# Feed-forward products moved 512 columns at a time, index queries rotated by ScalarE copies, and the recurrence's last steps one weight piece later

## The reference

```python
def swiglu(x, w_gate, w_up, w_down):            # 1024 -> 2816 -> 1024
    return (jax.nn.silu(x @ w_gate) * (x @ w_up)) @ w_down

# in each of the two last layers
q, k, v, ga, iq, ik, iw, xr, gr, ma, mb = jnp.split(h @ w_in[l], offsets, axis=-1)
iq = apply_rope(iq.reshape(B, S, 16, 64), cos_i, sin_i)   # [x1*c - x2*s, x2*c + x1*s]
ik = apply_rope(ik, cos_i, sin_i)
# index scores of iq and ik choose the keys of the attention
hr = rg_lru(causal_depthwise_conv_2(xr), ...)   # a recurrence over the tokens
y_b = (hr * jax.nn.silu(gr)) @ w_out_rnn[l]
merged = jax.nn.sigmoid(ma) * y_a + jax.nn.sigmoid(mb) * y_b
```

## Time and profile before

| | |
|---|---|
| median of 3 runs | 2159.14 us (2158.46 to 2160.78) |
| the profiled execution | 2158.18 us |
| its span in the trace | 2156.3 us |
| PE busy | 2111.6 us, 98% of the span |
| DVE, ACT, POOL busy | 1730.8, 1487.3, 394.1 us |
| TensorE clock granted | full in all 40 slices of the page |

### The profile page before, as it was taken

One profiled execution on the slowest core, in us unless ns is written; L12 is line 12 of the kernel. 1 busy time (PEld: TensorE's weight loads), 2 busy tenths in 40 slices (PEclk: granted clock), 3 DMA queues, 4 the chain that ended last, 5 costly groups with the idle time before them and its releaser, 6 DMA issues.

```text
span 2156.3 us, 33385 instructions
## 1 busy us (share of the span) xinstructions
PE 2111.6 (98%) x13067; PEld 1839.3 (85%) x13067; DVE 1730.8 (80%) x2150; ACT 1487.3 (69%) x1986; POOL 394.1 (18%) x354
## 2 busy tenths in 40 slices
PE   8999999989999999999999999999999999999998
PEld 8888999878888888888888888878899888999877
DVE  6756555879999999999999999985699666689775
ACT  5644444666887888888888888864578845468964
POOL 1511000001011000000000000000658600367820
PEclk9999999999999999999999999999999999999999
DMA  8225956429999999999999999985656465555561
GB/s 284 97 68 129 276 179 183 158 101 359 353 370 387 395 387 393 383 389 378 385 357 393 374 388 377 375 318 166 181 169 194 150 230 178 172 179 177 172 209 61
DMA packets 297421, 564.62 MB, mean 262 GB/s; under 512 B 19600, under 2 KB 113576, under 8 KB 297256
## 3 DMA queue, kind: packets, MB, share of 16 engines
q1 hardware_dynamic: 285328, 527.60, 69.3%
q0 software_dynamic: 11824, 34.77, 5.8%
q10 hardware_dynamic: 104, 0.04, 0.0%
HBM read 548.32 MB, written 14.02 MB: 261 GB/s over the span
## 4 chain that ended last, share of the span: by engine, by line
PE 75%; POOL 11%; DVE 4%; issue 4%; ACT 2%; DMA 2%; SPq 1%; POOLq 0%; DVEq 0%; ACTq 0%
PE bank L951 23%; PE bank L953 23%; PE bank L952 23%; POOL work L910 5%; POOL work L914 3%; PE bank L957 2%; POOL work L905 2%; DMA work<-in_w_ig_dram 1%; PE bank L1128 1%; DVE parts L2845 1%; POOL work L896 1%; DMA raw<-in_a_w_in_dram 0%; POOL work L894 0%; DVE work L2984 0%; DVE cols L2899 0%
## 5 line engine op out<-in xcount | busy, mean ns | idle before, releaser
L2845 DVE TENSOR_TENSOR parts<-raw,parts 128x1024 fp32r<-128x1024 f32 x701 | 851.1, 1229 | 307.7 <-ACT parts L2094 282.9
L2094 ACT CAST parts<-raw 128x1024 fp32r<-128x1024 f32 x701 | 731.0, 1047 | 411.7 <-PE bank L953 387.5
L951 PE MATMUL bank<-cols,parts 128*128 128x256 f32 x1376 | 398.8, 290 | 0.0
L952 PE MATMUL bank<-cols,parts 128*128 128x256 f32 x1376 | 389.8, 283 | 0.0
L953 PE MATMUL bank<-cols,parts 128*128 128x256 f32 x1376 | 389.8, 283 | 0.0
L2845 DVE TENSOR_TENSOR fast<-raw,fast 128x1024 fp32r<-128x1024 f32 x302 | 361.5, 1217 | 24.7 <-ACT fast L2094 7.7
L2094 ACT CAST fast<-raw 128x1024 fp32r<-128x1024 f32 x302 | 316.3, 1052 | 84.4 <-PE bank L953 77.0
L951 PE MATMUL bank<-parts,cols 128*128 128x512 f32 x868 | 344.2, 397 | 3.2 <-DVE cols L2899 1.9
L953 PE MATMUL bank<-parts,cols 128*128 128x512 f32 x868 | 338.5, 390 | 0.0
L952 PE MATMUL bank<-parts,cols 128*128 128x512 f32 x868 | 338.2, 390 | 0.0
L951 PEld LDWEIGHTS bank<-cols,parts 128*128 128x128 f32 x1376 | 263.7, 192 | 6.1 <-issue 4.6
(11 more groups left out here) (454 smaller groups left out, 3066.7 us busy)
## 6 DMA issues: line engine op xcount, KB each, us to landing
raw<-in_moe_w_gate_dram SPq DMA_DIRECT2D x112, 1024.0 KB, 9.0
raw<-in_moe_w_up_dram SPq DMA_DIRECT2D x112, 1024.0 KB, 8.5
raw<-in_moe_w_down_dram SPq DMA_DIRECT2D x112, 1024.0 KB, 9.1
raw<-in_w_in_dram SPq DMA_DIRECT2D x76, 1024.0 KB, 5.3
raw<-in_a_w_in_dram SPq DMA_DIRECT2D x11, 1024.0 KB, 11.7
raw<-in_ffn_w_gate_dram SPq DMA_DIRECT2D x11, 1024.0 KB, 5.4
raw<-in_ffn_w_up_dram SPq DMA_DIRECT2D x11, 1024.0 KB, 5.4
raw<-in_ffn_w_down_dram SPq DMA_DIRECT2D x11, 1024.0 KB, 5.2
```

The source lines that it names most:

```text
L951: pe.matmul(o, l[0], r[0], start=start, stop=False)
L952: pe.matmul(o, l[0], r[1], start=False, stop=False)
L2094: a.copy(dst[0], src).then_inc(*up(o + "hi", x))
L2845: v.tensor_tensor(dst[1], src, dst[0].bitcast(F32), ALU.subtract).then_inc(*up(o + "lo", x))
```

## The change

Three edits.

1. **Feed-forward.** XT's two parts are laid side by side (`XT_both`, 8 x 512 columns). Per row block there is one product of the high weights with all 512 columns and one of the low weights with the 256 high columns. Gate and up get a bank each (`N2.banks`). DVE adds the two halves of each bank (`tensor_reduce`, event `h_sum`) into SBUF; silu and the multiplication read SBUF; rounding (`h_hi`) and low part (`h_lo`) move behind the next block's first piece. The first block keeps its products.
2. **Index queries.** PE's `rope` and DVE's `rope` go. ACT makes four copies of 32 partitions per pair (`index_swaps`), driven by the pairs of the iq pieces, DVE uses `swapped`. The exchange matrix loses its sign, the sine tables get it (two more small DVE operations, once). The side task keeps its number of steps, so the index scores stand at the same steps.
3. **Recurrence.** `behind_mb` ticks behind (0, 2), (1, 0), (1, 2), (1, 3), on PE, ACT and DVE.

```diff
-    XT = tuple(v3(cols_[:, i, :], 8) for i in range(2))
+    XT_both = v3(cols_[:, :, :].rearrange("p a b -> p (a b)"), 8)
+    XT = tuple(XT_both[:, :, i * T:(i + 1) * T] for i in range(2))
...
-    N2.sg = v3(take(2 * T), 2)
+    N2.sg, N2.up = v3(take(2 * T), 2), v3(take(2 * T), 2)
...
+    N2.banks = lambda nb, q: 4 + 2 * (nb % 2) + q
...
-                b = 4 + nb % 4
                 if nb == 0:
-                    two_by_parts(0, b, *T_gu[0])
+                    two_by_parts(0, 4, *T_gu[0])
+                    busy[4] = ("h", 0)
                 for q in range(2 if nb else 0):
                     x = T_gu[nb][q]
                     _, w = piece_view(W, x)
+                    b = N2.banks(nb, q)
                     pe.wait_ge(*at(lo_name(x), x))
-                    if q == 0:
-                        claim(b)
+                    claim(b)
                     for k in range(8):
-                        k_ = mm3(bank[b][:, q * T:(q + 1) * T], sl(w, ALL, k), sl(XT, ALL, k), k == 0, k == 7)
+                        pe.matmul(bank[b][:, :], w[0][:, k], XT_both[:, k, :], start=k == 0, stop=False, skip_group_check=True)
+                        k_ = pe.matmul(bank[b][:, 0:T], w[1][:, k], XT[0][:, k], start=False, stop=k == 7, skip_group_check=True)
                     k_.then_inc(*up("used", x))
-                busy[b] = ("h", nb)
+                    busy[b] = ("h_sum", nb, q)
...
-                def rope(Xt, n, rotc, name, odd=0, l=l):
-                    for i in range(0, n, 2):
-                        m = min(2, n - i)
-                        b = 4 + (i // 2 + odd) % 2
-                        claim(b)
-                        pe.matmul(bank[b][:, 0:m * T], rotc, Xt[:, i:i + m, :].rearrange("p a b -> p (a b)"), start=True, stop=True).then_inc(*up("rot", l, name, i))
-                        busy[b] = ("rot_sin", l, name, i)
-                        yield
...
-                    pe.wait_ge(*at("iq", l, 6))
-                    yield
-                    yield from rope(L2.IQ, 8, C(C_ROTI), "iq")
-                    yield
+                    for _ in range(6):
+                        yield
...
-                    if q % 2:
+                    if (c, q) in ((0, 2), (1, 0), (1, 2), (1, 3)):
                         tick()
...
@@ ACT
+        def h_hi(gi, j, nb):
+            a.wait_ge(*at("h", nb))
+            if j == 0:
+                a.wait_ge(*at("used", T_dn[gi - 2][-1] if gi > 1 else T_aout[-1]))
+            a.copy(N2.hT[gi % 2][0][:, j, :], N2.sg[:, nb % 2, :]).then_inc(*up("h_hi", nb))
...
-                for x in T_gu[nb]:
-                    after(x)
                 s_ = N2.sg[:, nb % 2, :]
-                a.wait_ge(*at("used", T_gu[nb][1]))
-                if nb > 1:
-                    a.wait_ge(*at("h_lo", nb - 2))
-                a.activation(s_, bank[4 + nb % 4][:, 0:T], ACT.Silu).then_inc(*up("h_silu", nb))
-                a.wait_ge(*at("h", nb))
-                if j == 0:
-                    a.wait_ge(*at("used", T_dn[gi - 2][-1] if gi > 1 else T_aout[-1]))
-                a.copy(N2.hT[gi % 2][0][:, j, :], s_).then_inc(*up("h_hi", nb))
+                after(T_gu[nb][0])
+                if j:
+                    h_hi(gi, j - 1, nb - 1)
+                after(T_gu[nb][1])
+                if nb:
+                    a.wait_ge(*at("h_sum", nb, 0))
+                    a.activation(s_, s_, ACT.Silu).then_inc(*up("h_silu", nb))
+                else:
+                    a.wait_ge(*at("used", T_gu[0][1]))
+                    a.activation(s_, bank[4][:, 0:T], ACT.Silu).then_inc(*up("h_silu", 0))
                 nb += 1
+            h_hi(gi, m - 1, nb - 1)
...
+                    next(iqs, None)
...
+                def index_swaps(l=l):
+
+                    yield
+                    for i in range(0, 8, 2):
+                        r_ = L2.rt[:, i // 2 % 2, :].rearrange("p (a b) -> p a b", a=2)
+                        a.wait_ge(*at("iq", l, i))
+                        if i > 2:
+                            a.wait_ge(*at("roped", l, "iq", i - 4))
+                        for p0, p1 in ((0, 32), (32, 0), (64, 96), (96, 64)):
+                            k = a.copy(r_[p0:p0 + 32], L2.IQ[p1:p1 + 32, i:i + 2, :])
+                        k.then_inc(*up("swap", l, "iq", i))
                         yield
...
-                fm(t_["iq"], to(L2.IQ, "iq", 2))
+                iqs = index_swaps()
+                fm(t_["iq"], to(L2.IQ, "iq", 2), pairs=iqs)
...
-                    if q % 2:
+                    if (c, q) in ((0, 2), (1, 0), (1, 2), (1, 3)):
                         tick()
...
@@ DVE
+        def h_lo(gi, j, nb):
+            v.wait_ge(*at("h_hi", nb))
+            v.tensor_tensor(N2.hT[gi % 2][1][:, j, :], N2.sg[:, nb % 2, :], N2.hT[gi % 2][0][:, j, :].bitcast(F32), ALU.subtract).then_inc(*up("h_lo", nb))
...
-                for x in T_gu[nb]:
-                    after(x)
-                s_ = N2.sg[:, nb % 2, :]
+                s_, u_ = N2.sg[:, nb % 2, :], N2.up[:, nb % 2, :]
+                for q, d in enumerate((s_, u_)):
+                    after(T_gu[nb][q])
+                    if q == 0 and j:
+                        h_lo(gi, j - 1, nb - 1)
+                    if nb:
+                        v.wait_ge(*at("used", T_gu[nb][q]))
+                        if q == 0 and nb > 1:
+                            v.wait_ge(*at("h_lo", nb - 2))
+                        v.tensor_reduce(d, bank[N2.banks(nb, q)][:, :].rearrange("p (a b) -> p b a", a=2), AX_X, ALU.add).then_inc(*up("h_sum", nb, q))
                 v.wait_ge(*at("h_silu", nb))
-                v.tensor_tensor(s_, s_, bank[4 + nb % 4][:, T:2 * T], ALU.mult).then_inc(*up("h", nb))
-                v.wait_ge(*at("h_hi", nb))
-                v.tensor_tensor(N2.hT[gi % 2][1][:, j, :], s_, N2.hT[gi % 2][0][:, j, :].bitcast(F32), ALU.subtract).then_inc(*up("h_lo", nb))
+                if nb:
+                    v.wait_ge(*at("h_sum", nb, 1))
+                v.tensor_tensor(s_, s_, u_ if nb else bank[4][:, T:2 * T], ALU.mult).then_inc(*up("h", nb))
                 nb += 1
+            h_lo(gi, m - 1, nb - 1)
...
-            v.tensor_scalar(sinA[0:64, :], sinA[0:64, :], -1.0, None, ALU.mult).then_inc(*up("sin_sign"))
+            for x in (sinA[0:64, :], sinI[0:32, :], sinI[64:96, :]):
+                v.tensor_scalar(x, x, -1.0, None, ALU.mult).then_inc(*up("sin_sign"))
...
+                def swapped(Xt, name, cos, sin, l=l):
...
-                        v.tensor_tensor(r_, r_, sinA.unsqueeze(1).broadcast_to([128, 2, T]), ALU.mult).then_inc(*up("dve"))
-                        v.tensor_tensor(x2, x2, cosA.unsqueeze(1).broadcast_to([128, 2, T]), ALU.mult).then_inc(*up("dve"))
+                        v.tensor_tensor(r_, r_, sin.unsqueeze(1).broadcast_to([128, 2, T]), ALU.mult).then_inc(*up("dve"))
+                        v.tensor_tensor(x2, x2, cos.unsqueeze(1).broadcast_to([128, 2, T]), ALU.mult).then_inc(*up("dve"))
...
-                def index_steps(l=l):
-                    v.wait_ge(*at("cos", 1))
-                    r_ = L2.rt[:, 1, 0:T]
+                def key_rope(l=l):
+                    r_ = L2.rl[:, 0, 0:T]
                     v.wait_ge(*at("rot", l, "ik", 0))
                     v.tensor_tensor(r_, bank[5][:, T:2 * T], sinI, ALU.mult).then_inc(*up("rot_sin", l, "ik", 0))
                     v.tensor_tensor(L2.IK, bank[5][:, 0:T], cosI, ALU.mult).then_inc(*up("ik_cos", l))
                     v.wait_ge(*at("ik_cos", l))
                     v.tensor_tensor(L2.IK, L2.IK, r_, ALU.add).then_inc(*up("roped", l, "ik", 0))
-                    v.wait_ge(*at("roped", l, "ik", 0))
-                    yield
-                    yield from rope(L2.IQ, 8, cosI, sinI, "iq")
+
+                def index_ropes(l=l):
                     yield
                     yield
+                    yield from swapped(L2.IQ, "iq", cosI, sinI)
+                def index_steps(l=l):
+                    key_rope()
+                    next(iqr, None)
+                    yield
+                    next(iqr, None)
+                    for _ in range(6):
+                        yield
...
-                fm(t_["iq"], None)
+                iqr = index_ropes()
+                fm(t_["iq"], None, pairs=iqr)
...
-                    if q % 2:
+                    if (c, q) in ((0, 2), (1, 0), (1, 2), (1, 3)):
                         tick()
...
-    main = [eye, np.ones((128, 128), f), rot(128), rot(64), (col <= row).astype(f), (row < col).astype(f),
+    main = [eye, np.ones((128, 128), f), rot(128), np.abs(rot(64)), (col <= row).astype(f), (row < col).astype(f),
```

More of the change, by code:

```diff
@@ L73 @@
     "dve_norm": ("add", "ln_mean", "ln_p", "ln_diag", "rows", "h_rows", "h_diag", "resid", "f_over", "final"),
-    "dve_ffn": ("h", "h_lo"),
+    "dve_ffn": ("h_sum", "h", "h_lo"),
     "dve_attention": ("over_sums", "masked", "nmax", "probs", "o_cols", "swa_k", "swa_v", "swa_q"),
@@ L3646, in layers @@
                 t_ = T_l[l]
```

(21 more changed lines are left out.)

## The result

The changed kernel takes 2148.83 us (median of 7 executions, 2144.68 to 2153.75) against 2158.46 (2155.09 to 2161.36): 0.9947 of the time before, 95% interval 0.9931 to 0.9964. It is faster, by 9.6 us where 14.7 were forecast, and inside the range. The profiled execution took 2145.25 us.

What follows compares the result with a forecast made beforehand. PE's own work was taken to set the time. Savings of 4.3 + 6.9 + 3.5 = 14.7 us gave a span of 2141.6, 2143.5 as whole execution and 2144.4 us as median, range 2140.5 to 2150.8.

Steps and rivals of the forecast that it cites:

- Part 1, 4.3 us: Feed-forward: 336 triples of 256-column products become one of 512 and one of 256, 0.360 to 0.347 us each.
- I take 0.347, made of the very sizes used: Feed-forward: a new pair costs 0.227 + 0.120 = 0.347 us, from rows of those two sizes.
- The rival that had two products of 768 columns at 0.360 us: Feed-forward wins nothing, as the pair costs what the triple did; only the layers gain: 2148.7 us, chance 0.08.
- The upper bound from the narrow pair (0.39): Feed-forward: alternation costs 0.07 us on top per pair, so the stage loses 10 us: 2159 us, chance 0.04.
- the 1.13 us worked out: Feed-forward: price per reduction up to which DVE's block still fits beside PE's 5.6 us.
- DVE's 18 to 19 us of four blocks: Feed-forward, sign of being right: four blocks take 22.2 us with DVE busy 18 to 19 us of it.
- Part 2, 6.9 us: Index queries: PE loses eight rotations of 0.86 us, 3.4 us per layer, with ACT's copies hidden from PE.
- POOL is tied to PE: Last layers: POOL waits for DVE scans behind PE's pieces, so its last tap should come 3.4 us earlier too.
- less than 6 us as a sign against the tie: Layer one, sign of being wrong: POOL's last tap comes less than 6 us earlier; near 1702.5 was right.
- Part 3, 3.5 us: Recurrence: group 7's matrices come one piece later, so PE's wait for POOL, 1.75 us, goes twice.
- DVE not waiting for hr's load: Recurrence, sign of being right: hr's load, 9.1 us to landing, comes in time, with 1.4 us of room left.
- the median shown is 1.0 above that execution: Whole kernel: 1.0 us from the profiled execution to the median, taking 2143.5 us to 2144.4 us.

Runs made afterwards that it cites:

- Grouped: Changed kernel with each feed-forward piece's eight 512-column products first and its eight 256-column ones behind: 2145.53 us, again 2145.29 us against 2148.81 for the changed kernel.
- this part alone: Kernel before with only the index-query hunks: 2157.73 us, ratio 0.999; once more 2152.37 us against 2157.8, ratio 0.9985.
- the second profile: The changed kernel run again without any edit: 2148.81 us, ratio 0.9937 to the kernel before; profiled span 2147.7 us.
- the repeated execution: Second run of the kernel before with only the index-query hunks: 2152.37 us against 2157.8, ratio 0.9985; profiled span 2148.2 us.

## Why the prediction was right, and where it was off

- **What bounds the kernel** was read rightly: PE's own products. Wherever PE's work shrank the end moved with it, and POOL's 11% of the chain were worth only the wait through which the chain entered it.
- **Part 1, 4.3 us: the term that was mis-sized.** The step that failed is "I take 0.347, made of the very sizes used". Measured 0.353, so (0.3600 - 0.3531) x 336 = 2.3 us, and 2.2 between the marks. The pair is made of the sizes used, but not in the order used: those rows were of streams of one size, and here the sizes alternate. Grouped, a pair takes 0.349 us and the stage wins 3.7 us. Of the 0.006 us missing 0.004 are thus the turns (1.5 us in all), and the other 0.002 are the one change of size that a grouped piece still has, since behind five products the distance is 0.227 again. The rival that had two products of 768 columns at 0.360 us was wrong as well. The upper bound from the narrow pair (0.39) was far off. In the earlier trace rows too the long distance, 0.17, is the one behind the larger product, so the guess that the short one doesn't cover a weight load doesn't follow from them; no run here shows why that pair is so dear.
- The Trainium skill, "TensorE: Matmul & The Clock Gate", section Back-to-back issue gap, gives columns / 2.4 + 2.5 ns between warm products (it calls this the gap of a product by itself), by estimate 325 ns for this pair. The trace has 353, and neither that rule nor the sum from rows of one size has a term for a change of size.
- **DVE in feed-forward.** 0.69 us per reduction was forecast and 0.683 measured. The room was there, and is wider than the 1.13 us worked out: 1.37 us cost 0.6 us in all. DVE's 18 to 19 us of four blocks came out as 15.7, for two reasons: three of the 24 operations counted (a reduction, a multiplication and a low part of the last block) fall behind the stretch's end, and the spans of neighbours overlap by some 0.1 us, so that the 21 add up to 17.2 us and cover 15.7.
- **Part 2, 6.9 us.** Measured 3.4 in each layer, 6.8. The copies took the forecast 0.62 us, and twice their price is hidden. By the medians this part alone gained 2.8 and 5.4 us. The wait of index scores for ACT stayed (1.3 us now, 1.7 before); that it moves by 0.3 to 0.7 us either way was within the 1 us given.
- **POOL follows.** The step "POOL is tied to PE" held: its last tap moved 5.16 us, PE's stream the same. I had put its end at 1702.5 and named less than 6 us as a sign against the tie. It came at 1705.1, not because the tie failed but because PE had gained only 5.2 us by then: 2.1 us less in feed-forward, and 0.1 from the clock and 0.3 at the scores. The test should have named PE's own shift at that point, not a time.
- **Part 3, 3.5 us.** Measured 1.8 in each layer. In other executions the wait that it removes was 0.6 us, since POOL's last tap takes 1.08 us or 1.78, so 0.8 to 1.8 per layer is its honest price. hr's load kept 1.2 us of room in the first layer (1.4 forecast) and 2.8 in the second, but landing takes 8.0 to 11.5 us, and "DVE not waiting for hr's load" failed in the second profile, by 0.5 us. Where DVE waited 2.6 us, PE lost 0.4.
- **The sum.** 2.2 + 6.8 + 3.6 + 0.4 (scores) make 13.0 us, and the spans differ by 12.84. Against 14.7 forecast 2 are missing in part 1. The rest of the distance from 2144.4 to the median of 2148.83 is the step "the median shown is 1.0 above that execution": after the change the profiled execution was one of the fastest, 3.6 us under the median of its kernel. Scatter of the clock had been given 1.5 us, and is more like 4.

## What to carry to other kernels

A chain's share of an engine says nothing of what is to be won there; the length of the wait through which the chain enters it does. When products are merged to save instructions, keep equal sizes together, as it cost nothing here and brought 1.5 us more, a third of the 4.3 that had been expected. And where each execution has its own stretches at half clock, measure a part between two marks of the same stream, and let the test of a mechanism be a shift against that stream rather than a point of time.

## What the runs showed that I had not expected

- **A change of size costs PE time in the products behind it**: coming from 256 columns, the first five products of 512 take 0.228 to 0.236 us from start to start and the next 0.227, at full clock and without a wait. In turns the pair takes 0.236 + 0.117 us, grouped 0.349 in sum.
- **POOL's two-input operation has no single price.** The same 88x506 tap took 1.08, 1.78 and 4.42 us. In the last case it lay from 2051.5 to 2055.9 beside DVE's low parts, 2.68 us for four and 2.35 us for two in one stretch:

```profile
2050.06 2.68 DVE L3818 TENSOR_TENSOR fast<-work,fast 128x512 fp32r<-128x512 f32 x4
2052.66 2.35 DVE L2849 TENSOR_TENSOR parts<-raw,parts 128x1024 fp32r<-128x1024 f32 x2
```

In the repeated execution its 1.08 us (from 2047.85) lay beside DVE's scan of the recurrence (2.17 us from 2047.88) and nothing else on DVE. The Trainium skill, "GPSIMD Engine Reference", section Specifications, has POOL's way to SBUF shared with VectorE, with contention where a DVE instruction reads two inputs from SBUF. That agrees with the 4.42 us, while the scan, which the kernel also gives two tiles of SBUF, did not lengthen the tap beside it; how much each DVE operation costs a tap, no run here isolates.
- **Near a wait of PE there can be a stretch at half clock**: 3.4 us of it 1.9 us behind a wait of 1.6, and 10.2 us that began in a wait of 7.0. It cost 1.7 us in the first case, as much as the wait, and 3.0 in the second. Eight of the ten waits had none near them, and that the waits brought the two about is not shown, so it is a risk and no fixed price.
